# The fourth gate chunk of each layer as seven products behind the recurrence, with four plain gates fewer between its levels

## The reference

```
def hybrid_mixer(h, w_in_l, ...):                     # h: 256 tokens x 1024 features
    (sq, sk, sv, dq, dk, dv, iq, ik, iw, hq, hf, hi, hg,
     g_sb, g_dsa, g_hg) = jnp.split(h @ w_in_l, ..., axis=-1)
    y_sb = stick_breaking_attention(sq, sk, sv) @ w_sb_l
    y_dsa = dsa_attention(...) @ w_dsa_l              # top-64 sparse attention
    o = hgrn2(hq, hf, hi, lb)                         # a gated linear recurrence in time
    y_hg = (rms_norm(o, onorm) * jax.nn.silu(hg)) @ w_hg_l
    mixed = (jax.nn.sigmoid(g_sb) * y_sb + jax.nn.sigmoid(g_dsa) * y_dsa
             + jax.nn.sigmoid(g_hg) * y_hg)
    return mixed @ w_out_l
```

## Time and profile before

| | |
|---|---|
| Time, median of 3 runs | 1598.94 us (1597.66 to 1599.24) |
| The profiled execution's own time | 1599.52 us |
| Its span, first to last instruction | 1597.7 us |
| PE busy | 1465.1 us (92%), 8156 matmul records |
| DVE busy | 740.9 us (46%) |
| ACT busy | 314.8 us (20%) |
| Levels of the recurrence, layer 0 | about 164 to 216 us of the span |
| The same, layer 1 | about 634 to 686 us |

### The profile page before, as it was taken

One profiled execution on the slowest core, in us unless ns is written; L12 is line 12 of the kernel. 1 busy time (PEld: TensorE's weight loads), 2 busy tenths in 40 slices (PEclk: granted clock), 3 DMA queues, 4 the chain that ended last, 5 costly groups with the idle time before them and its releaser, 6 DMA issues.

```text
span 1597.7 us, 19690 instructions
## 1 busy us (share of the span) xinstructions
PE 1465.1 (92%) x8156; PEld 1006.0 (63%) x8156; DVE 740.9 (46%) x1465; ACT 314.8 (20%) x655; POOL 22.7 (1%) x41
## 2 busy tenths in 40 slices
PE   8999999999999999999999999999999576576578
PEld 5587889999544788898999445755554133133132
DVE  3646576766666646567666656544331000001001
ACT  2234431122001125430222001334410000000000
POOL 0000000000000000000000002200000000000000
PEclk9999999999999999999999999999999788788789
DMA  9547224454443633334444446755799999999997
GB/s 321 187 159 237 95 101 153 161 182 179 158 167 110 218 130 135 106 106 158 158 161 181 186 158 196 232 185 184 288 381 425 427 427 425 428 427 426 427 419 313
DMA packets 114921, 380.17 MB, mean 238 GB/s; under 512 B 10836, under 2 KB 23252, under 8 KB 104144
## 3 DMA queue, kind: packets, MB, share of 16 engines
q1 hardware_dynamic: 111952, 369.53, 60.7%
q0 software_dynamic: 2880, 9.36, 1.9%
HBM read 377.25 MB, written 5.73 MB: 240 GB/s over the span
## 4 chain that ended last, share of the span: by engine, by line
PE 32%; DMA 17%; SPq 1%; DVE 0%; ACT 0%; issue 0%; DVEq 0%
DMA ring<-in_w 17%; PE bank L1495 6%; PE bank L1541 6%; PE bank L1151 4%; PE bank L1692 4%; PE bank L1261 2%; PE bank L1590 2%; PE bank L1718 1%; SPq L928 1%; PE bank L1751 1%; PE bank L1187 1%; PE bank L1213 1%; PE bank L1200 1%; PE bank L1714 1%; PE bank L1648 0%; PE bank L1681 0%
## 5 line engine op out<-in xcount | busy, mean ns | idle before, releaser
L1144 PE MATMUL bank<-hT,ring 128*128 128x256 f32 x832 | 185.4, 381 | 0.0
L1144 PEld LDWEIGHTS bank<-hT,ring 128*128 128x128 f32 x832 | 156.0, 190 | 21.9 <-issue 1.0
L1692 PE MATMUL bank<-ring,region 128*32 128x512 f32 x208 | 115.7, 720 | 50.2 <-DMA region<-in_w 50.2
L1692 PE MATMUL bank<-region 128*32 128x512 f32 x512 | 115.8, 720 | 42.9 <-DMA ring<-in_w 42.9
L1541 PE MATMUL bank<-region 128*128 128x512 f32 x320 | 140.6, 592 | 0.0
L1541 PEld LDWEIGHTS bank<-region 128*128 128x128 f32 x320 | 60.5, 190 | 74.6 <-issue 74.6
L1495 PE MATMUL bank<-region 128*128 128x128 f32 x768 | 100.5, 275 | 0.0
L1495 PEld LDWEIGHTS bank<-region 128*128 128x128 f32 x768 | 93.0, 192 | 0.0
L1692 PEld LDWEIGHTS bank<-region 128*32 128x32 f32 x512 | 28.8, 129 | 87.4 <-issue 87.4
L1692 PEld LDWEIGHTS bank<-ring,region 128*32 128x32 f32 x208 | 25.7, 129 | 85.0 <-issue 85.0
L1751 PE MATMUL bank<-region 128*32 128x512 f32 x192 | 61.9, 748 | 15.7 <-DMA hT<-in_w 13.9
(11 more groups left out here) (486 smaller groups left out, 2413.7 us busy)
## 6 DMA issues: line engine op xcount, KB each, us to landing
region<-in_w SPq DMA_DIRECT2D x43, 2048.0 KB, 38.6
ring<-in_w SPq DMA_DIRECT2D x30, 2048.0 KB, 37.5
ring<-in_w_in SPq DMA_DIRECT2D x26, 2048.0 KB, 8.4
ring<-in_w_up SPq DMA_DIRECT2D x16, 2048.0 KB, 8.3
ring<-in_w_down SPq DMA_DIRECT2D x32, 1024.0 KB, 6.4
own_slot<-in_w SPq DMA_DIRECT2D x7, 2048.0 KB, 43.5
ring<-in_w_out SPq DMA_DIRECT2D x6, 2048.0 KB, 7.8
region<-in_w SPq DMA_DIRECT2D x22, 512.0 KB, 9.0
```

The source lines that it names most:

```text
L1144: t = mm(b[:, 0:T], w[:, k, :], act[:, k, :], start=(k == 0), stop=(k == KD - 1))
L1692: t = mm(b[32 * e:32 * e + 32, :], xg[:, k, 32 * e:32 * e + 32], four[e][c][:, 512 * (k % 2):512 * (k % 2) + 512], start=(k == 0), stop=(k ...
```

## The change

Gate chunk 3 is made as seven products too: it becomes the first of the three late chunks, and chunks 4 and 5 follow it. Its four plain gates go: twelve plain gates are left, and between the levels there is one behind each of levels 0 to 4 and none behind levels 5 and 6. The quarter sums of chunk 3 lie where those of `hf` lay; those of chunk 4 keep their place, and so do those of chunk 5, by the new condition. The semaphore counts follow (three chunks of seven products per layer became four). The new list puts chunk 3 where chunk 4 stood (with the attention steps between its products), chunk 4 behind it as a piece, then chunk 5 as before. The line numbers of the kernel after are higher by one from line 225 on.

```
-LATE_GATES = 8
+LATE_GATES = 12
...
-SEVENS = ("hf", 4, 5)
+SEVENS = ("hf", 3, 4, 5)
...
-        s += g(2 if j < 2 else 1)
+        s += g() if j < 5 else []
...
-    s += [("gt",), ("gw", 4), ("ho",)]
-    s += att[18:20] + gm(4, 0, *GATE_ORDER[:4]) + [att[20], ("on",), att[21]] + gm(4, 0, *GATE_ORDER[4:])
-    s += [("gw", 5), ("gc", 4, 0)] + att[22:] + gm(4, 1, *GATE_ORDER) + [("gc", 4, 1), ("gs",), ("gf", 4, 0), ("gf", 4, 1)]
+    s += [("gt",), ("gw", 3), ("ho",)]
+    s += att[18:20] + gm(3, 0, *GATE_ORDER[:4]) + [att[20], ("on",), att[21]] + gm(3, 0, *GATE_ORDER[4:])
+    s += [("gw", 4), ("gc", 3, 0)] + att[22:] + gm(3, 1, *GATE_ORDER) + [("gc", 3, 1), ("gs",), ("gf", 3, 0), ("gf", 3, 1)]
+    s += gm(4, 0, *GATE_ORDER) + [("gw", 5), ("gc", 4, 0), ("gf", 4, 0)] + gm(4, 1, *GATE_ORDER) + [("gc", 4, 1), ("gf", 4, 1)]
...
         def gate_sums(l, c):
             own_, a21 = own_quarters, gate_weights(l, c)[1][0]
-            if c in ("hf", 4):
+            if c != 4:
                 return own_[:, 0], own_[:, 1], a21, own_[:, 2]
             return own_[:, 3], low_quarters[:, 0], a21, low_quarters[:, 1]
...
-                    elif m == "m5" and c in ("hf", 4):
-                        pe.wait_ge(row_sums_ready, 2 * l + 1 + (c == 4))
+                    elif m == "m5" and c in ("hf", 3):
+                        pe.wait_ge(row_sums_ready, 2 * l + 1 + (c == 3))
```

More of the change, by code:

```diff
@@ L1301, in gate_product @@
                         arrived((l, seven_chunk(c)))
-                    elif m == "m5" and c in ("hf", 4):
-                        pe.wait_ge(row_sums_ready, 2 * l + 1 + (c == 4))
+                    elif m == "m5" and c in ("hf", 3):
+                        pe.wait_ge(row_sums_ready, 2 * l + 1 + (c == 3))
                     if m in GATE_ORDER[2:6]:
-                        pe.wait_ge(quarter_sums_ready, 12 * l + 4 * SEVENS.index(c) + GATE_ORDER.index(m) - 1)
+                        pe.wait_ge(quarter_sums_ready, 16 * l + 4 * SEVENS.index(c) + GATE_ORDER.index(m) - 1)
                 if m in GATE_STARTS:
@@ L2444, in gate_weight_sums @@
                 s1, s2, s3, s4 = gate_sums(l, c)
-                n = 12 * l + 4 * SEVENS.index(c)
+                n = 16 * l + 4 * SEVENS.index(c)
                 V.tensor_tensor(s1, a21, a22, ALU.add).then_inc(quarter_sums_ready, 1)
@@ L2462, in gate_corner_sums @@
             def gate_corner_sums(l, c, t2):
-                n = 6 * l + 2 * SEVENS.index(c) + t2
+                n = 8 * l + 2 * SEVENS.index(c) + t2
                 if n >= 2:
@@ L2598, in _ @@
                             if m < 2:
-                                dve.wait_ge(seven_sigmoids, 6 * l + m + 1)
+                                dve.wait_ge(seven_sigmoids, 8 * l + m + 1)
                             t = V.tensor_scalar(fT[:, m, :], fT[:, m, :], omlb[:, l, m:m + 1], lb[:, l, m:m + 1],
@@ L2731, in _ @@
                     if m % 4 == 0:
-                        dve.wait_ge(seven_sigmoids, 6 * l + 4 + m // 2)
+                        dve.wait_ge(seven_sigmoids, 8 * l + 6 + m // 2)
                     ga = gT.rearrange("p (b m) t -> p b m t", b=3)
```

## The result

The changed kernel takes 1611.73 us (median of 4 runs, 1610.63 to 1614.89) against 1598.57 of the kernel before beside it (4 runs, 1597.66 to 1599.24): 13.2 us more, a ratio of 1.0085 with a 95% interval of 1.0073 to 1.0097. The forecast was 1611.1 us, 12.2 more. The profiled execution is the longest of the four (1614.89 us, span 1613.0), so its own account is for 1614.89 - 1599.52 = 15.4 us.

A forecast was written before the change was run, and what follows sets the result against it. PE was taken to bound the levels, with DVE close behind. 2 x (12.5 added - 7.8 won back) = +9.4 us, plus 2.8 us of clock, made +12.2 us: 1611.1 us, range 1604 to 1618.

The forecast's parts named there:

- (a): Behind levels 0 and 1: one gate less at each comes back whole, 7.0 us a layer, without PE waiting for DVE.
- (b): Gate behind level 5: removal gains only 0.05 us, as PE then waits some 3.4 us for DVE before level 6.
- (c): Gate behind level 6: output products start 2.97 us earlier, but PE gains 0.8 us at most, waiting at the last transposes.
- What the added chunk costs: Chunk 3 as products, behind the levels: 12.5 us a layer, all on PE's path, with DVE's added work hidden.
- The shift is carried to the end: Expert stage: its DMA slots are freed by PE's progress, so every microsecond of PE's path in the layers reaches the end.
- The clock: Behind the new PE waits in the layers: the clock falls for a time, costing 1.4 us a layer, +2.8 us in all.
- this wait of 2.2 us: Sign: before the last transposes of the attention, PE waits some 2.2 us for DVE's normalisation, ended by L2232.
- the six rows: Six expert-stage PE waits used to price the clock: losses of 0 to 2.3 us each, 1.4 in the mean.
- the held clock: Rival: the clock stays up through both gaps in the layers, giving 1608.3 us; chance 0.27.
- DVE bounding every level: Rival: gates behind levels 0 and 1 win nothing either, +25 us, 1623.9 us; chance 0.08.
- all gates coming back: Rival: DVE's chain runs early enough, so a layer wins 14.0 us for 12.5, giving 1595.9 us; chance 0.04.
- the second block hiding it: Rival: expert-stage loads begin at a time PE does not set, so the lost time vanishes, 1598.9 us; chance 0.03.

The follow-up runs named there:

- e7: Changed kernel with its twelve plain gates moved: none behind levels 0 and 1, one behind each of levels 2 to 6; 1611.74 us, +13.2 against the kernel before.
- e1: Changed kernel with one plain gate made a second time behind level 5, filling the wait there; 1608.30 us, +9.3 against the kernel before.
- e2: Removal alone: kernel before without the four plain gates, nothing in place of chunk 3 (stand-ins for its gate tiles); 1588.78 us, -10.2.
- e3: Addition alone: kernel before with chunk 3 also made as seven products, all sixteen plain gates kept; 1624.51 us, +25.5.
- e9: Changed kernel with a plain gate kept behind level 6, none behind level 5, one fewer behind `u`; 1604.80 us, +5.7 against the kernel before.
- e5: e1 with the last transposes of the attention moved behind four more products; 1605.41 us, +6.8 against the kernel before.
- e6: Changed kernel, gates one fewer behind `u`, one behind levels 0 to 5; e5's move; one DVE normalisation behind level 4's multiply; 1597.30 us, -1.3 against kernel before.
- e4: Changed kernel with its twelve plain gates moved: one behind every level 0 to 6, two fewer ahead of the levels; 1597.96 us, -1.1 against the kernel before.
- e8: e4 with one DVE normalisation moved behind the multiply of level 4; 1596.86 us, -2.3 against the kernel before.

## Why the prediction was right

Its sum was right: +12.2 forecast, +13.2 measured. By its steps:

- *What the removed gates bring.* (a) holds: no wait at levels 1 and 2, and -6.91 us to level 6 where 7.05 was worked out. The limit next to it is shown by e7. (b) holds: the wait of 3.41 us, ended by L2679, and e1 puts the gate back at no cost. (c) holds as a mechanism: e1's layer 1 shows the second wait, 1.89 us for the forecast 2.2 (PE waits 0.72 us for the merge before the output products there, and so comes later), and layer 1 of e2 shows it with the same 1.89.
- *What the added chunk costs.* 12.50 us from the last transposes to the branch projection, as worked out; DVE's part is hidden; e3 measures 25.5 for 25.0.
- *The shift is carried to the end.* 15.4 us at the span's end, 7.2 + 8.2 in the layers.
- *The clock: the term that was mis-sized.* The step read "I take 1.4 us a layer". By the medians it is (13.2 - 9.4) / 2 = 1.9 us. In the profiled execution, the longest, it is 7.2 - 4.7 = 2.5 us in layer 0 and 8.2 - 4.7 = 3.5 us in layer 1, net of the wait at the last transposes, which the slow stretch took up whole: this wait of 2.2 us, announced as a sign, did not appear there. The first branch projections came 7.9 and 16.1 us later (0.7 us of each from ahead of the change), where 4.7 to 7 and twice that were announced. By the prediction's own formula, (1 - c) times the length, that execution lost 5.1 and 6.8 us of clock (0.7 of the latter while PE waited), where the largest of the six rows gave 2.3. The number came out near because some 2 us of each loss fell where PE would have waited, which is partly luck: the prediction names this offset but gives it no size. With another order behind the same wait of 3.41 us, e9 lost 0.9 us a layer. What I left out is that the loss behind a wait of one length varies this much; layers 0 and 1 of e2 show it with one order of work (13.7 us, and twice 3.4), and what settles it stays open.

The Trainium skill (TensorE: Matmul & The Clock Gate, HAM oscillation) has bursts behind such waits start at half rate. The trace agrees in part: behind the wait of 3.41 us the clock was low in both layers of the change and of e2 and in layer 0 of e9, but in layer 0 of the change the burst began at 1.00 and the clock fell some 1.4 us into it, and in layer 1 of e9 it did not fall. As a price by the largest rows it gave 14.0 us, 0.8 over the 13.2 where the sum taken lies 1.0 under it.

Of the rivals, the held clock (1608.3) is refuted by the windows of the change; its number was met by e1, where the clock nearly held, with the schedule's 9.4 us. DVE bounding every level (1623.9, or 1622.3 with the 0.8 us of (c), which its price leaves out), all gates coming back (1595.9) and the second block hiding it (1598.9) are out by the rows above.

Still open is why layer 0 loses clock where layer 1, with the same order of work, does not (e1, e5, e6, e9), or loses less (e2), while in the change layer 1 loses more.

## What to carry to other kernels

Price a piece of filler work by the slack of the engine behind it at that very place: of two gates in a gap one was cover, worth next to nothing to remove, and the other was worth its whole 3.5 us, and the same four removals gave 14 us a layer by the list but 7.8 by the slack. When a removal opens a wait on the matmul engine, price the clock as a range and not from one trace: behind one wait of 3.41 us it was low for anything from 0 to nearly 14 us, and the two layers of e2, with one order of work, had 13.7 and 2 x 3.4 us. So take filler away where little waits (here ahead of the levels) before taking it from between dependent steps.

## What the runs showed of the hardware

- Behind the same wait of 3.41 us the granted clock was at 0.50 for some 10 us (layer 0 of the change), 13.7 us (layer 1 of it, and layer 0 of e2) and 3.4 us (layer 1 of e2) with a wait of 0.47 us and output products of 128x64 behind it, and for 3.4 and 0 us (e9) with a 128x256 gate behind it. PE was busy for nearly all of the time behind the waits.
- Shorter waits were followed by a slow stretch too: 2.83 us in both layers of e7; and 0.72 us, with the output products behind it, in layer 0 of e1, e5 and e6 (3.4 us each), but not in their layers 1. In e4 and e8, where a gate stands there and PE does not wait, the same products ran at 1.00 in both layers.
- A slow PE is not always lost time: in the change some 2 of the 3.94 us by which the output products and the first two products took longer would have been a wait (1.89 us in layer 1 of e1).
